# Transformer block pair on one core: near bias as skewed slices, head norms beside the value projection, plain scores, a reordered end of the first attention

## The reference

```
q, k, v, u = split(rmsnorm(x) @ w_in)                    # 4 x 512 columns
q, k = per-head rmsnorm of q and k                       # 8 heads of 64
s = q @ k.T * 64**-0.5 + rel_bias[:, clip(qpos - kpos, -128, 128) + 128]
a = softmax(s where the key's chunk is not later) @ v    # 64-token chunks
p = (trailing means over 2, 4, 8, 16 tokens of u, minus u) @ pool_w * pool_scale
x = x + concat(a, p) @ w_out
```

## Time and profile before

| | us |
|---|---|
| runs | 1574.46, 1574.64, 1576.36; median 1574.64 |
| profiled execution | 1575.12 |
| its span (first to last instruction) | 1573.0 |
| PE busy | 1542.8 (98%) |
| DVE busy | 744.6 (47%) |
| ACT busy | 569.5 (36%) |
| POOL busy | 79.8 (5%) |
| DMA queue of SP | 141.58 MB, 30.5% of 16 engines |

### The profile page before, as it was taken

How to read it: one execution, slowest core, us unless ns; L and a number is a source line. 1 busy time by engine, 2 the same in 40 slices (tenths; PEclk the granted TensorE clock), 3 DMA queues, 4 the chain that set the end, 5 groups by cost and what they waited for, 6 DMA issues and landing times.

```text
span 1573.0 us, 19156 instructions
## 1 busy us (share of the span) xinstructions
PE 1542.8 (98%) x7150; PEld 1247.6 (79%) x7150; DVE 744.6 (47%) x1076; ACT 569.5 (36%) x933; POOL 79.8 (5%) x66
## 2 busy tenths in 40 slices
PE   8999999999999899999999999999999999999998
PEld 7888888877876688888888878766788888888886
DVE  5444432456365564444323474575554643234434
ACT  6222312235146443222212273255644433124322
POOL 0000000002013110000000051100000000000000
PEclk9999999999999999999999999999999999999999
DMA  6333343333221233333333343321132332233322
GB/s 191 96 93 94 94 107 93 94 107 114 81 67 41 58 103 99 102 93 93 96 103 95 93 108 91 112 65 52 57 125 77 94 93 94 94 97 98 100 94 94
DMA packets 246025, 147.65 MB, mean 94 GB/s; under 512 B 17472, under 2 KB 230096, under 8 KB 245840
## 3 DMA queue, kind: packets, MB, share of 16 engines
q1 hardware_dynamic: 232896, 141.58, 30.5%
q10 hardware_dynamic: 13072, 5.31, 1.4%
HBM read 142.66 MB, written 4.21 MB: 93 GB/s over the span
## 4 chain that ended last, share of the span: by engine, by line
PE 92%; DVE 3%; ACT 2%; issue 1%; DMA 1%; POOL 0%; SPq 0%; DVEq 0%; ACTq 0%; POOLq 0%
PE bank L345 29%; PE bank L348 28%; PE bank L349 28%; DVE w_low L1110 1%; PE bank L2235 1%; ACT w_high L591 1%; PE bank L2050 1%; PE bank L2037 1%; PE bank L2351 0%; PE bank L2348 0%; PE bank L2181 0%; PE bank L2140 0%; DMA region_f<-in_x 0%; DMA w_raw<-in_w_out 0%; PE bank L1955 0%
## 5 line engine op out<-in xcount | busy, mean ns | idle before, releaser
L345 PE MATMUL bank<-region,w_high 128*128 128x512 f32 (+2 forms) x1492 | 586.9, 393 | 6.5 <-DVE w_low L1110 1.9
L349 PE MATMUL bank<-region,w_low 128*128 128x512 f32 (+2 forms) x1492 | 579.8, 389 | 0.0
L348 PE MATMUL bank<-region,w_high 128*128 128x512 f32 (+2 forms) x1492 | 579.6, 388 | 0.0
L1110 DVE TENSOR_TENSOR w_low<-w_raw,w_high 128x1024 fp32r<-128x1024 f32 (+1 forms) x259 | 334.6, 1299 | 150.0 <-ACT w_high L591 146.2
L591 ACT CAST w_high<-w_raw 128x1024 fp32r<-128x1024 f32 (+1 forms) x259 | 265.6, 1027 | 265.0 <-DMA w_raw<-in_ffn_w_down 107.3
L345 PEld LDWEIGHTS bank<-region,w_high 128*128 128x128 f32 (+1 forms) x1492 | 279.9, 188 | 70.6 <-DVE w_low L1110 6.8
L349 PEld LDWEIGHTS bank<-region,w_low 128*128 128x128 f32 (+1 forms) x1492 | 279.8, 188 | 60.1
L348 PEld LDWEIGHTS bank<-region,w_high 128*128 128x128 f32 (+1 forms) x1492 | 280.1, 188 | 56.5
L345 PE MATMUL bank<-w_high,region 128*128 128x512 f32 x416 | 165.1, 397 | 2.5 <-DVE w_low L1110 1.5
L349 PE MATMUL bank<-w_high,region 128*128 128x512 f32 x416 | 162.9, 392 | 0.0
L348 PE MATMUL bank<-w_low,region 128*128 128x512 f32 x416 | 162.5, 391 | 0.0
(11 more groups left out here) (259 smaller groups left out, 1130.4 us busy)
## 6 DMA issues: line engine op xcount, KB each, us to landing
w_raw<-in_ffn_w_down SPq DMA_DIRECT2D x48, 512.0 KB, 4.0
w_raw<-in_ffn_w_gate SPq DMA_DIRECT2D x44, 512.0 KB, 3.8
w_raw<-in_ffn_w_up SPq DMA_DIRECT2D x44, 512.0 KB, 3.8
w_raw<-in_w_in SPq DMA_DIRECT2D x40, 512.0 KB, 3.9
w_raw<-in_w_up SPq DMA_DIRECT2D x32, 512.0 KB, 4.0
w_raw<-in_w_down SPq DMA_DIRECT2D x32, 512.0 KB, 3.3
w_raw<-in_w_out SPq DMA_DIRECT2D x16, 512.0 KB, 3.8
region_f<-in_x SPq DMA_DIRECT2D x4, 512.0 KB, 7.2
```

Source lines behind the costliest of these rows:

```text
L345: mm = pe.matmul(out, a_hi, b_hi, start=start, stop=False)
L348: pe.matmul(out, a_hi, b_lo, start=False, stop=False)
L349: return pe.matmul(out, a_lo, b_hi, start=False, stop=stop)
L1110: last = dve.tensor_tensor(piece(w_low[b % RING]), piece(w_raw[b % RING]), piece(w_high[b % RING]).bitcast(F32), ALU.subtract)
```

## The change

- Bias: DVE writes each head's near bias backwards into rows of 384; ACT stores them and then stores all eight rows 128 times over into a DRAM tensor (1.57 MB) after tile 1 of the first down stage. A head's band is two DMAs whose rows start one element earlier from partition to partition (bias_load, 64 rows of 192 and 64 of 256). Heads 0 to 3 are loaded ahead of the q/k projection, 4 to 7 in steps 5, 6, 9, 10 of the loop. PE's a_bias, ACT's bias_copy and toeplitz go. DVE's memsets of the bias tiles move from before the loop into the first FFN.
- Head norms: sums 5, 6 and 7 after value steps 0 and 1, transposes after step 2, the wait for the rows after step 3; spreads in twos. ACT's copy of head_select moves to q/k tile 3. DVE writes the normed q and k in float32; there are no high parts and remainders.
- Scores: one float32 product per head in place of three.
- Loop: sixteen steps. u tile 2 is emptied at the end of DVE's step 8. Pair 1's output is split after the loop.
- End: pool products in banks 3 to 6, mixed with the last pair's weighing (a_weigh_cols), transposes and inverse sums; DVE's and ACT's orders follow.

Cut to its core, indented eight less; the bodies of a_bias, toeplitz, bias_copy, qk_norm_lo and of the three old loops over the pool products are removed and left out here.

```diff
-def plain_keys(c, k):
-    first = 5 * (3 - k) if c else 6 * k + 1
-    return plain[:, first:first + TT - k, :].rearrange("p b n -> p (b n)")
+def plain_keys(c, k, q0=None, q1=TT):
+    first = (5 * (3 - k) if c else 6 * k + 1) - k
...
         if n == 0:
             act.wait_ge(rel_padded, 1)
-            act.dma_start(rel_pad_dram, rel_rows[:]).then_inc(rel_stored, 16)
+            act.dma_start(rel_pad_dram, rel_back[:]).then_inc(rel_stored, 16)
+        if n == 1:
+            act.wait_ge(rel_stored, 16)
+            one = rel_pad_dram[0:1, 0:1].copy()
+            act.dma_start(rel_rep_dram, bass.AP(one.tensor, one.offset, [[0, P], [1, HEADS * REL_ROW]])).then_inc(rel_repeated, 16)
     def split_hi(b, it=None, step=0):
...
+    def bias_load(h):
+        if h >= 4:
+            act.wait_ge(a_biased, 2 * TT * (h // 2 - 1))
+        for row0, width in ((0, 192), (64, 256)):
+            at = REL_ROW * h + P - 1 - row0
+            first = rel_rep_dram[row0:row0 + 1, at:at + 1].copy()
+            skew = bass.AP(first.tensor, first.offset, [[HEADS * REL_ROW - 1, 64], [1, width]])
+            act.dma_start(bias[row0:row0 + 64, h % 4, 256:256 + width], skew).then_inc(bias_in[h % 4], 16)
+    act.wait_ge(rel_repeated, 16)
...
+        bias_load(h)
     act.wait_ge(lam_summed, 1)
...
-    act.copy(head_select[:], const[:, C_HROW:C_HROW + 2 * S]).then_inc(select_made, 1)
     for i in range(8):
         split_hi(BLK["qk"] + i + AHEAD)
         if i == 0:
             head("m1")()
+        if i == 3:
+            act.copy(head_select[:], const[:, C_HROW:C_HROW + 2 * S]).then_inc(select_made, 1)
         act.wait_ge(acc_free, RES["qk"] + i + 1)
         if i >= 2:
             act.wait_ge(h_stat, i - 1)
         act.activation(head_sq[:, i % 2, :], qk_raw[:, i, :], ACT.Square).then_inc(y_sq, 1)
-    for i in range(3):
-        split_hi(BLK["v"] + i + AHEAD)
+    split_hi(BLK["v"] + AHEAD)
     act.wait_ge(h_stat, 8)
     act.activation(head_std[:], bank[4][:, 0:TT * 2 * HEADS], ACT.Sqrt, scale=1.0 / 64, bias=eps_col[:]).then_inc(h_std, 1)
+    split_hi(BLK["v"] + 1 + AHEAD)
     act.wait_ge(h_turned, 1)
     act.wait_ge(select_made, 2)
     act.copy(head_rows[0:2 * HEADS, :], bank[5][0:2 * HEADS, :]).then_inc(h_rows_hi, 1)
-    for i in range(8):
...
         act.wait_ge(a_normed, p + 1)
         act.copy(part[1][:, p, :], a_full[:, p % 2, :]).then_inc(a_ohi, 1)
-    for w in range(2 * HEADS + 2):
+    for w in range(2 * HEADS):
         p, q = divmod(w, TT)
         for c in range(2):
-            if w < 2 * HEADS:
-                a_expo(2 * w + c)
-            if c == 0 and 1 <= w <= 2 * HEADS:
+            a_expo(2 * w + c)
+            if c == 0 and w >= 1:
                 a_turned_even(w - 1)
-        if w < 2:
-            toeplitz(w + 2)
-        if q >= 2 and 2 * p + q < HEADS:
-            bias_copy(2 * p + q)
-            if 2 * p + q + 2 < HEADS:
-                toeplitz(2 * p + q + 2)
+        if w in (5, 6, 9, 10):
+            bias_load(2 * p + q + 1)
         if w >= 5 and q == 1:
             a_spread_copy(p - 1)
-        if w >= 10 and q == 2:
-            a_pair_hi(p - 2)
+        if w == 10:
+            a_pair_hi(0)
         if w in (5, 8, 12):
             pooled_hi((5, 8, 12).index(w))
         if w in (1, 4, 8, 12):
             split_hi(BLK["u"] + (1, 4, 8, 12).index(w) + AHEAD)
-    pooled_hi(3)
-    a_pair_hi(2)
-    a_pair_hi(3)
-    split_hi(BLK["poolw"] + AHEAD)
-    for j in range(4):
+    def pool_out_hi(j):
         g = 3 - j
         act.wait_ge(acc_ready, RES["poolw"] + j + 1)
-        act.activation(part[1][:, 4 + j, :], bank[(RES["poolw"] + j) % BANKS][:], ACT.Identity,
-                       scale=pool_gain[:, g:g + 1]).then_inc(ev_hi, 1)
+        act.activation(part[1][:, 4 + j, :], pool_bank(j)[:], ACT.Identity, scale=pool_gain[:, g:g + 1]).then_inc(ev_hi, 1)
+    pooled_hi(3)
+    a_pair_hi(1)
+    pool_out_hi(0)
+    a_turned_even(2 * HEADS - 1)
+    a_spread_copy(3)
+    a_pair_hi(2)
+    pool_out_hi(1)
+    pool_out_hi(2)
+    split_hi(BLK["poolw"] + AHEAD)
+    pool_out_hi(3)
+    a_pair_hi(3)
     for n in range(DT):
         split_hi(BLK["out1"] + n + AHEAD)
         act.wait_ge(acc_free, RES["out1"] + n + 1)
...
         dve.wait_ge(const_in, 16)
-        dve.tensor_copy(far[:], rel_rows[:, 256:257]).then_inc(far_copied, 1)
-        dve.memset(rel_rows[:, 257:384], 0.0)
+        dve.tensor_copy(far[:], rel_rows[:, N_REL - 1:N_REL]).then_inc(far_copied, 1)
+        dve.memset(rel_back[:, 0:REL_ROW - N_REL], 0.0)
         dve.wait_ge(far_copied, 1)
-        dve.tensor_scalar(rel_rows[:, 0:257], rel_rows[:, 0:257], far[:], None, ALU.subtract).then_inc(rel_padded, 1)
+        last = rel_rows[:, N_REL - 1:N_REL].copy()
+        backwards = bass.AP(last.tensor, last.offset, [list(last.ap[0]), [-1, N_REL]])
+        dve.tensor_scalar(rel_back[:, REL_ROW - N_REL:], backwards, far[:], -1.0, ALU.subtract, ALU.mult).then_inc(rel_padded, 1)
+        for s_ in range(4):
+            link(dve.memset(bias[0:64, s_, 448:512], BIG))
+            ins = dve.memset(bias[:, s_, 0:256], 0.0)
+        ins.then_inc(bias_cleared, 1)
     def small_products():
...
     lam_finish()
     dve.tensor_copy(head_rows[:], const[:, C_HROW:C_HROW + S]).then_inc(select_made, 1)
-    for i in range(3):
-        split_lo(BLK["v"] + i + AHEAD)
+    split_lo(BLK["v"] + AHEAD)
     dve.wait_ge(h_std, 1)
     dve.reciprocal(head_rstd[:], head_std[:]).then_inc(h_rec, 1)
+    split_lo(BLK["v"] + 1 + AHEAD)
     dve.wait_ge(h_rows_hi, 1)
     dve.tensor_tensor(head_rows[32:32 + 2 * HEADS, :], bank[5][0:2 * HEADS, :], head_rows[0:2 * HEADS, :].bitcast(F32),
                       ALU.subtract).then_inc(h_rows_lo, 1)
...
     for i in range(8):
-        if i == 2:
-            split_lo(BLK["v"] + 3 + AHEAD)
+        if i in (2, 4):
+            split_lo(BLK["v"] + 1 + i // 2 + AHEAD)
         dve.wait_ge(h_bc, i + 1)
-        if i >= 2:
-            dve.wait_ge(qk_lo, i - 1)
-        dve.scalar_tensor_tensor(qk_full[:, i % 2, :], qk_raw[:, i, :], qk_gain[:, i // 4:i // 4 + 1],
+        dve.scalar_tensor_tensor(over[1][:, i, :], qk_raw[:, i, :], qk_gain[:, i // 4:i // 4 + 1],
                                  bank[6 + i % 2][:], ALU.mult, ALU.mult).then_inc(qk_full_ready, 1)
-        if i > 0:
-            qk_norm_lo(i - 1)
-    qk_norm_lo(7)
     for i in range(TT):
         acc = result(RES["v"] + i)
         dve.tensor_scalar(over[2][:, i, :], acc[:], r_col[:, i:i + 1], None, ALU.mult).then_inc(acc_free, 1)
...
         n = (q + 1) * P
         dve.wait_ge(a_score, u + 1)
         if q == 0:
-            dve.wait_ge(b_done, h + 1)
+            dve.wait_ge(bias_in[h % 4], 32 * (h // 4 + 1))
         if u >= 2:
             dve.wait_ge(a_exp, u - 1)
         dve.tensor_tensor_reduce(out=a_s[:, u % 2, 0:n], in0=bank[4 + u % 2][:, 0:n],
...
         dve.tensor_tensor(u_pad[:, 3 - j, PAD:], acc[:], rstd[:], ALU.mult).then_inc(acc_free, 1)
     u_tile(0, bank[5])
-    for s_ in range(4):
-        link(dve.memset(bias[:, s_, 0:256], 0.0))
-        link(dve.memset(bias[0:64, s_, 448:512], BIG))
-    for w in range(2 * HEADS + 2):
+    for w in range(2 * HEADS):
         p, q = divmod(w, TT)
-        if w in (4, 9, 14):
+        if w in (4, 14):
             u_tile(w // 5 + 1, bank[3])
         if w >= 5 and q == 1:
             a_invert(p - 1)
-        if w < 2 * HEADS:
-            a_min_of(2 * w)
-            a_min_of(2 * w + 1)
-        if 1 <= w <= 2 * HEADS:
+        a_min_of(2 * w)
+        a_min_of(2 * w + 1)
+        if w >= 1:
             a_turned_odd(w - 1)
+        if w == 8:
+            u_tile(2, bank[3])
         if w >= 9 and q == 1:
             a_norm(p - 2)
-        if w >= 10 and q == 2:
-            a_pair_lo(p - 2)
+        if w == 10:
+            a_pair_lo(0)
         if w in (5, 8, 12):
             pooled_lo((5, 8, 12).index(w))
         if w in (1, 4, 8, 12):
             split_lo(BLK["u"] + (1, 4, 8, 12).index(w) + AHEAD)
+    def pool_out_lo(j):
+        g = 3 - j
+        dve.wait_ge(acc_ready, RES["poolw"] + j + 1)
+        dve.wait_ge(ev_hi, 3 + j + 1)
+        dve.scalar_tensor_tensor(part[1][:, 12 + j, :], pool_bank(j)[:], pool_gain[:, g:g + 1], part[1][:, 4 + j, :].bitcast(F32),
+                                 ALU.mult, ALU.subtract).then_inc(acc_free, 1)
+    a_norm(2)
+    a_invert(3)
+    pooled_lo(3)
+    a_pair_lo(1)
+    a_turned_odd(2 * HEADS - 1)
+    pool_out_lo(0)
+    a_pair_lo(2)
+    pool_out_lo(1)
+    pool_out_lo(2)
     a_norm(3)
-    pooled_lo(3)
-    a_pair_lo(2)
+    split_lo(BLK["poolw"] + AHEAD)
+    pool_out_lo(3)
     a_pair_lo(3)
-    split_lo(BLK["poolw"] + AHEAD)
...
     for n in range(DT):
         acc = result(RES["out1"] + n)
         dve.tensor_tensor(x[:, n, :], acc[:], x[:, n, :], ALU.add).then_inc(acc_free, 1)
...
     columns("qk", 8, x_in1, after_qk, need=lambda k: pe.wait_ge(xt_lo, GEN["m1"] + k + 1),
```

(67 more changed lines are left out.)

83 lines of the change are left out of this document (19 added, 64 removed).

## The result

| | before | after |
|---|---|---|
| median of 4 runs on one chip, us | 1575.50 | 1560.21 |
| lowest to highest | 1574.46 to 1578.22 | 1560.05 to 1560.87 |
| profiled execution | 1575.12 | 1560.29 |
| its span | 1573.0 | 1558.3 |

The ratio is 0.9902, with a 95% interval of 0.9886 to 0.9917. The direction was right. Lines of kernel.py move with the change: the three products of split3 are L345, L348, L349 in the kernel before and L348, L351, L352 in the changed one.

A forecast was written before the change was run, and what follows sets the result against it. TensorE (PE), holding 92% of the chain, was taken to bound the kernel. Terms 4.0 + 3.9 - 1.3 + 0.9 + 3.35 = 10.85 us off 1575.12 gave 1564.3, said as 1564 for the median; range 1561 to 1569.

The forecast's parts named there:

- the likeliest case: The whole kernel's forecast of 1564 us, own range 1562 to 1566, chance 0.50.
- Rival E: More is gained: no stall at the attention's end, no eviction wait; 1561 to 1562 us, chance 0.07.
- Part 1: Head norms beside value projection: waits of 1.4 and 1.3 us go, clock gives 1.5, switch costs 0.2; 4.0 us gained.
- The clock term: Behind the head norms' sums of squares: granted clock no longer falls, 1.5 us gained, bounds 0 and 1.65.
- Part 2: Bias without PE: gap before first scores 2.0, eviction wait -0.75, six head biases in loop 2.65; 3.9 us gained.
- rival D: Skewed loads land late, DVE waits at loop steps 8 and 12; slower, 1581 us if landing takes 16; chance 0.05.
- Rival C: At the start, root late again or eight issues hold the projection's square root; 3 us stay, 1567 us, chance 0.09.
- Part 3: Attention loop: one plain score product is dearer than three; 1.3 us lost over four pairs, lower bound 0.9.
- Rival B: Loop scores cost a third more, 3.6 us in place of 1.3; 1566 us, chance 0.10.
- Part 4: Attention loop's own waits of 0.4 and 0.5 us go; 0.9 us gained, bounds 0 and 0.9.
- rival A: Half given back: clock falls, ACT and DVE pace the loop, end stalls, 1.5 us each; 1568 to 1570, chance 0.16.
- Part 5: Attention's end: four waits of 4.2 us filled, less 0.35 for switches and 0.5 idle; 3.35 us gained, bounds 1.5 and 3.9.

The follow-up runs named there:

- experiment 1: 32 bytes per partition put ahead of f3_rest alone or all FFN scratch: kernel before 1571.82 or 1572.06 us, changed kernel 1563.28 or 1563.57 us.
- experiment 7: Kernel before with one float32 score product per head and no high parts and remainders of q and k, nothing else of the change: 1576.54 us, ratio 1.0013.
- experiment 3: Changed kernel with sums of squares 5, 6 and 7 together again behind value step 1: 1562.99 us, ratio 0.9908.
- experiment 5: Changed kernel with DVE's eight bias-tile memsets back between the first u tile's eviction and the first minimum: 1560.77 us, ratio 0.9903.
- Experiment 6: Changed kernel with PE's order at the end straightened, pool product 0 behind weighing, transposes and spread; ACT's and DVE's orders kept: 1561.38 us, ratio 0.9909.
- before_plain_scores: Kernel before with one float32 score product per head and q and k written once in float32, all else in place: 1576.54 us, ratio 1.0013.

## Why the prediction was wrong, and where it was right

**The step that failed is the sum's scope.** It added up the changed stages and took everything behind them as unchanged, without a reason given. What a tensor's new address does to the products of a later stage was no term and no rival. It is 3.15 us in the profiles, confirmed from both sides by experiment 1. Without it the changed kernel takes 1563.3, inside the likeliest case's own range. The changed stages gave 1.5 to 1.7 us more than forecast besides; these alone would have stayed inside the range. Rival E (1561 to 1562) had the right direction and the wrong cause: the eviction's wait stayed at 0.4 us and the end's idle at 0.27.

**Part 1, head norms: right, a little small.** Waits gone, clock kept, root in time, each as forecast. Sum 4 to the first scores gained 6.87, where 4.0 + 2.0 = 6.0 was forecast. The clock term was 1.5 and measured 1.59. Most of the rest comes from pricing two terms by the list of waits and not, as the prediction says itself, by starts. The transposes and the first spreads, then the lone spread, in the kernel before:

```profile
441.72 0.60 PE L1963 MATMUL bank<-const,head_rstd 128*16 128x128 f32 x4
443.70 0.73 PE L1988 MATMUL bank<-head_rows,head_select 128*128 128x512 f32 x2 [1.38 <-DVE head_rows L1271]
444.27 0.39 PE L345 MATMUL bank<-w_high,region 128*128 128x512 f32 x1
...
450.01 0.39 PE L349 MATMUL bank<-w_high,region 128*128 128x512 f32 x1
451.66 0.51 PE L1988 MATMUL bank<-head_rows,head_select 128*128 128x512 f32 x1 [1.26 <-DVE qk_full L1283]
```

By starts, the first place took 2.55 us, and 0.82 in the changed kernel: 1.7 gained and not 1.4. The second lost 1.4 (1.65 where 0.23 is the rule) and not 1.3. With 1.6 for the clock and 2.05 for the gap before the scores that is 6.8 of the 6.87. One reason was off: the 1.3 us of qk_full was put down to the split and the hand-over alike, and experiment 7 shows that the hand-over's end alone brings back 0.1 of it. And two terms were not as independent as the sum has them: the fall of the clock hid a late root (experiment 3).

**Part 2, bias without PE: right.** The gap before the scores closed, and the eviction became late next at 0.8 us (first step 2.86 instead of 2.05 us; 0.75 forecast). The memsets were hidden in the first FFN, as said. The loads land in 2.4 us, so rival D, which needed 12.7, was far off. The store of the repeated rows cost PE nothing: from the first weight product to q/k it took 362.8 us, 362.7 before. The only new wait there is the one of r_col. That one is the term mis-sized: eight issues were priced at 0.51 and nothing on PE, and took 0.62 each, 5.0 us. The root came 2.8 us later in its stage instead of 2.0, which overdrew a slack of 2.2; the wait is 0.51, and the stretch is 0.82 longer, inside the stated bound of 1. The sign for it, a spread that starts after 386, came true (387.44 us), though 1.3 us of that are the later start of the whole stretch. Rival C fell as a whole, with only this part of it true.

**Part 3, plain scores: right, slightly too dear.** 1.3 was taken with a lower bound of 0.9; the changed kernel shows 1.2. The steps of its loop that hold no bias and no wait are 0.07 us shorter than before at width 128, 0.09 longer at 256 and 0.12 at 384, and the 512 row says 0.16: 0.3 a pair. The narrow widths are the reason: 0.40 us for four widths came from scaling the 512 row, while at width 128 the prediction's own 0.42 against 0.49 already said slightly cheaper. Rival B is refuted. The four-pass rule of the Trainium skill, FP8 and Floating Point Precision, section TensorE Precision Notes, would have made it 3.6; this case's traces do not bear that out as a price against three reduced products (1.06 against 0.90 us at width 512).

**Part 4, the loop: right in the sum, short by 1.0.** Predicted for first to last scores: -0.75 + 2.65 - 1.3 + 0.9 = 1.5; measured 2.50. The scores explain 0.3 of the difference: they cost 1.0 of their 1.2 in this stretch, which ends where the last ones start. Some 0.9 are waits: the list has 0.4 + 0.5, but by starts steps 1, 2, 3 and 9 gain 0.35, 0.4, 0.3 and 0.8 beyond the bias and score products. The eviction takes 0.1 back. The 0.4 of step 2 (from the scores of w = 2 to those of w = 3: 3.59 us before, 2.88 after) is the wait for a_min. DVE had the weight split ahead of that minimum, and it took 2.19 us beside an operation of POOL; in the changed kernel POOL's starts when the split is nearly done. Before, then after:

```profile
471.18 1.27 POOL L1779 TENSOR_TENSOR u_pad<-win,u_pad 128x512 f32<-128x512 f32 x1
471.35 2.19 DVE L1110 TENSOR_TENSOR w_low<-w_raw,w_high 128x1024 fp32r<-128x1024 f32 x1 [1.81 <-ACT w_high L591]
```

```profile
467.29 1.31 DVE L1110 TENSOR_TENSOR w_low<-w_raw,w_high 128x1024 fp32r<-128x1024 f32 x1 [1.71 <-ACT w_high L598]
468.48 1.29 POOL L1784 TENSOR_TENSOR u_pad<-win,u_pad 128x512 f32<-128x512 f32 x1
```

Nothing in the change arranges this; as far as the 0.4 hangs on it, it is luck. The memsets, which the prediction names, hold 0.4 over steps 0 to 3 (experiment 5); what holds steps 1 and 3 beyond that is not shown. The pace held without bias work on PE, so the 1.5 us that rival A gave to ACT and DVE did not come.

**Part 5, the end: right, 0.6 small.** The stretch gives 4.02, and 3.9 with the idle behind it taken off and the 0.16 of the last scores, which part 3 counts, put back: against 3.35. The idle behind the pool remainder is 0.27 instead of 0.5, in the place and for the reason named. The rest is about the 0.35 held for the switches, which no run separates. Experiment 6 shows that PE's order is worth 1.0, mostly by the wait that it keeps out of the first output tile.

Rival A needed the clock, the loop and the end to give back 4.5 us in sum; none of its three did.

## What to carry to other kernels

A change that adds or drops a tensor moves all that lie behind it: compare the durations of untouched groups before crediting or blaming the edit, and try a pad ahead of a large streamed operand. Price each instruction that moves past a queue, DMA issues included, against the slack of the next thing that queue owes to PE. Small waits that remain can be read off the list of PE's waits and filled with work that is ready, but below 2 us it takes the trace and not the time to see it.

## What the runs showed of the hardware that was not expected

- The place of a streamed float32r operand in SBUF: 389 ns against 392 to 397 per 128x512 product, 3.2 to 4.5 us over the stage. Good at 0, 256 and 512 bytes from the changed kernel's place, bad at 32, 64, 96 and 128. Products of the other operand that PE takes in turn with it, and that did not move, lengthen too (389 to 397 ns at 32 bytes).
- A skewed DMA of 64 rows took ACT 0.62 us to issue at the median (0.45 at the least), where the two loads of the earlier trace rows took 0.51 each and the eight old ones 0.33 at the median.
- Subtractions on DVE took 1.68 instead of 0.69 us and 2.19 instead of 1.31 us where a tensor-tensor operation of POOL ran beside them (519.37 us in before_plain_scores, 471.35 us in the kernel before).
- The start of the q/k stretch varied from 375.7 to 377.5 us between profiles of kernels that do the same work before it.
- The lower clock comes and goes between profiles in stages that no edit touches: 0.91 in 925 to 945 us in one profile and 1.00 in another. Where it fell, PE had waited 1.3 us and then run 1.95 us of one-column sums of squares (933.47 to 935.42 in the changed kernel), the same kind of work that the change took apart in the head norms. Nothing was tried there.
